# State-space stage of a hybrid encoder kernel: the rounding of the turns and the scaling of the output matrices done on ScalarE in small operations

## The chip, the cores and the metric

One Trainium2 chip, one of its cores. The metric is device time in microseconds (us) for one execution of the whole kernel. Engines are named as in the profile: PE is TensorE (PEld its weight loads), DVE is VectorE, ACT is ScalarE, POOL is GpSimd, SP is SyncE, which here only issues transfers.

## The reference, cut to what matters

The block runs a bidirectional S5 state-space mixer and windowed attention side by side over 272 tokens, merges them by gates, and then runs a product-key expert network. The change is in the state-space mixer alone:

```
def _s5_direction(u_g, a_re, a_im, bb_re, bb_im, c_re, c_im, reverse):
    bu_re = jnp.einsum('lgc,gpc->lgp', u_g, bb_re)
    bu_im = jnp.einsum('lgc,gpc->lgp', u_g, bb_im)
...
    _, _, h_re, h_im = lax.associative_scan(
        _complex_linear_combine, (ar, ai, bu_re, bu_im), reverse=reverse, axis=0)
...
    return jnp.einsum('lgp,gcp->lgc', h_re, cr) - jnp.einsum('lgp,gcp->lgc', h_im, ci)
```

There are 64 groups of 64 states in each of two directions, 8,192 complex states in all. All arithmetic is in 32-bit floats.

## The kernel before, in words

**How the recurrence is turned real.** A complex state that decays by r and turns by an angle at each token is the same as a real recurrence with factor r on inputs that have been turned back by the angle times the token number; the result is turned forward again. So for each set of states the kernel needs the cosine and sine of (turn x token number). The turn is kept in revolutions: ACT multiplies the row of token numbers (`iota`) by the turn per state (tile `tb`), and DVE takes the nearest whole number away, by adding MAGIC (1.5 x 2^23, which leaves only whole numbers) and subtracting it again (tiles `rnd`, `ang`). ACT then makes sine and cosine of `ang` (tile `trig`).

**Tiling.** The 8,192 states stand as 64 columns of 128 partitions. The 1,024 channels are 8 channel tiles (`CT`), with 8 columns each. Columns go in pairs, so there are 32 pairs, 4 for each channel tile (`PPC`), and I call the work on one pair a step. The step function of each engine is unrolled 8 times in `scan_body`; the first body stands by itself, the other three are a hardware loop.

**One step on DVE**, in the order of the code: `pair` (multiply the projected inputs by cosine and sine, L852 and L853; real part of an older pair, L887; add and subtract, L858 and L859; four scans, L868), then `angles` (L838 and L840), `turned_back` (L879 and L880), and in three of the four steps of a channel tile a part of `out_matrices`. That function scales the output matrices C by the coefficients of the tile: four products of 128x256 numbers (L822, L823 in the tile's first step, L825, L826 in its second; tile `cs`), and two differences (L830, L831; tile `cp`) in its third. At a tile's first step stand also `scalars` (L800, L802: the tile's coefficients `scur` and channels `ucur`) and `inputs_low` (L807, L808).

**One step on ACT**: `turns` (L468, L469), `cos_sin` of the pair before (L477, L478, L480), at a tile's first step `inputs_high` (L491, L493), and `gate` (L487), which moves the gate projection of three steps ago out of the accumulator.

**One step on PE**: 8 matmuls of a gate projection (`half_gate`, L1206), the 12 that project the inputs to a pair's states (`state_inputs`, L1252, which wait for the multiplies of the pair before to have read the accumulator, L853), the 6 of `state_outputs` (L1266), and 8 more of the gate projection. In the profile's rows each matmul of L1206 and L1266 counts twice, so a step has 32 of the one and 12 of the other, and 12 of L1252.

**The order** is the order of the code on each engine; the engines meet by counting semaphores. `angles` of a step waits for `turns` of it (`s_tb`). `cos_sin` waits for DVE's `turned_back` of the step before (`s_oc`, `s_os`), and its result (`s_trg`) is used by DVE a step later. PE's `half_gate` waits for ACT's `gate` of two projections before (`s_gs`). SP loads weights into a ring of four, and B and C of a channel tile (`bwt`, `cwt`) ahead of it.

Of the kernel before, what the change touches and what calls it, by code (L numbers as in the profile page):

```python
# [19 lines left out]
ALU = mybir.AluOpType  # L20
ACT = mybir.ActivationFunctionType
AX_X = mybir.AxisListType.X

P = 128
# [3 lines left out]
L = META + SEQ  # L28
# [4 lines left out]
SPC = NST // CT  # L33
# [7 lines left out]
MAGIC = 1.5 * 2.0 ** 23  # L41
# [18 lines left out]
def build(nc, W, keys, par, bw, cw, meta, x, gffn, gfin, u_tab, v_tab, out):  # L60
    top = ExitStack()
    with top:
        def sem(name):
            return top.enter_context(nc.semaphore(name))

        def sbt(stack, name, shape, dt=F32):
            return stack.enter_context(nc.sbuf_tensor(name, shape, dt))
# [17 lines left out]
        hs2 = sbt(top, "hs2", [P, TT, D])  # L85
        st = sbt(top, "st", [P, 16])
        halfpi = sbt(top, "halfpi", [P, 1])


        mix = ExitStack()  # L90
# [17 lines left out]
        scur = sbt(mix, "scur", [P, 2, NSC, SPC])  # L108
# [3 lines left out]
        cwt = sbt(mix, "cwt", [P, 2, SPC, 2, 32])  # L112
# [6 lines left out]
        scan = ExitStack()  # L119
        bwH = sbt(scan, "bwH", [P, 2, 2, 2, P], F32R)  # L120
        cp = sbt(scan, "cp", [P, 2, 2, SPC, 32])
        cs = sbt(scan, "cs", [P, 4, SPC, 32])
        tb = sbt(scan, "tb", [P, 2, 2, L])
        rnd = sbt(scan, "rnd", [P, 2, L])
        ang = sbt(scan, "ang", [P, 2, 2, L])
        trig = sbt(scan, "trig", [P, 2, 2, 2, L])
        pa = sbt(scan, "pa", [P, 2, 2, L])
# [49 lines left out]
        def col(name, a=0, b=None):  # L177
            lo, hi = COLS[name]
            return prm[:, lo + a:hi if b is None else lo + b]

        ident = col("ident")
        iota = col("iota")
# [48 lines left out]
        s_cw = [sem("s_cw0"), sem("s_cw1")]  # L231
        s_scur, s_cpl = sem("s_scur"), sem("s_cpl")
        s_inH, s_inL = sem("s_inH"), sem("s_inL")
        s_cp = sem("s_cp")
        s_bu = sem("s_bu")
        s_tb, s_abs, s_trg, s_rnd = sem("s_tb"), sem("s_abs"), sem("s_trg"), sem("s_rnd")
        s_ang = sem("s_ang")
        s_ab = sem("s_ab")
        s_gin = sem("s_gin")
# [3 lines left out]
        s_y = sem("s_y")  # L243
# [27 lines left out]
        PPC = SPC // 2  # L271
# [6 lines left out]
        def behind(b, t, k):  # L278

            return (b, t - k) if t >= k else (b - 1, t - k + PPL)  # L280
# [5 lines left out]
        def units(t):  # L286

            cc, way, jp = place(t)
            return slice(4 * jp + way, 4 * jp + way + 3, 2)
# [90 lines left out]
        def _(act):  # L380
# [2 lines left out]
            act.sem_inc(s_qT[0], 1)  # L383
            act.sem_inc(s_qT[1], 1)
            act.sem_inc(s_gs, 2)
            act.sem_inc(s_h2T, 4)
            act.sem_inc(s_qp, 2)
            act.sem_inc(s_psc, 2)
# [72 lines left out]
            def turns(b, t):  # L461
                n = PPL * b + t
                cc = t // PPC
                if t % PPC == 0:
                    act.wait_ge(s_scur, 2 * (2 * b + cc) + 2)
                act.wait_ge(s_ang, n + 1)
                at = units(t).start
                nc.scalar.activation(tb[:, t % 2, 0, :], iota, ACT.Copy, scale=scur[:, cc, 0, at:at + 1])  # L468
                nc.scalar.activation(tb[:, t % 2, 1, :], iota, ACT.Copy, scale=scur[:, cc, 0, at + 2:at + 3]  # L469
                                     ).then_inc(s_tb, 1)  # L470

            def cos_sin(b, t):
                s, n = t % 2, PPL * b + t
# [9 lines left out]
            def gate(b, t):  # L483

                g = SPC * b + t
                act.wait_ge(s_wdone, RING + W_GATE + 1 + g)
                nc.scalar.activation(flat(gates_v[:, bass.ds(g, 1), :]), ps[:, t % 2, 0:SEQ], ACT.Identity,  # L487
                                     bias=prm[:, bass.ds(COLS["bgate"][0] + g, 1)]).then_inc(s_gs, 1)

            def inputs_high(b, cc):  # L490
                nc.scalar.activation(uP[:, cc, 0, :], ucur[:, cc, :], ACT.Copy).then_inc(s_inH, 1)  # L491
                act.wait_ge(s_bw[cc], 16 * b + 16)
                nc.scalar.activation(bwH[:, cc, :, :, :].rearrange("p d r s -> p (d r s)"),  # L493
                                     bwt[:, cc, :, :, :].rearrange("p d r s -> p (d r s)"), ACT.Copy).then_inc(s_inH, 1)

            def scan_body(b, first=False):
                for t in range(PPL):
                    turns(b, t)
                    if t >= 1 or not first:
                        cos_sin(*behind(b, t, 1))  # L500
                    if t % PPC == 0:
                        inputs_high(b, t // PPC)
                    if t >= LAG + 1 or not first:
                        gate(*behind(b, t, LAG + 1))

            scan_body(0, first=True)
            with act.Fori(1, BODIES) as b:
                scan_body(b)
# [9 lines left out]
            part = GATES * SEQ // CT  # L518
# [114 lines left out]
        def _(dve):  # L633
# [12 lines left out]
            def step(ins):  # L646

                n_v[0] += 1
                ins.then_inc(s_v, 1)
                dve.wait_ge(s_v, n_v[0])  # L650

            step(nc.vector.memset(halfpi[:, :], HALF_PI))
            nc.vector.memset(st[:, :], 1.0).then_inc(s_ms, 1)

            def low(n, i=0):
# [153 lines left out]
                                        bwt[:, cc, :, :, :].rearrange("p d r s -> p (d r s)"),  # L809
                                        bwH[:, cc, :, :, :].rearrange("p d r s -> p (d r s)"), ALU.subtract).then_inc(s_inL, 1)  # L810

            def out_matrices(b, cc, part):

                ct = 2 * b + cc
                cre, cim = cwt[:, cc, :, 0, :], cwt[:, cc, :, 1, :]

                def co(k):
                    return scur[:, cc, k, :].rearrange("p (i o) -> p i o", o=1).broadcast_to([P, SPC, 32])
                if part == 0:
                    dve.wait_ge(s_cw[cc], 16 * b + 16)  # L820
                    dve.wait_ge(s_cp, 2 * ct + 4)
                    nc.vector.tensor_tensor(cs[:, 0], cre, co(2), ALU.mult).then_inc(s_cpl, 1)  # L822
                    nc.vector.tensor_tensor(cs[:, 1], cim, co(3), ALU.mult).then_inc(s_cpl, 1)  # L823
                elif part == 1:
                    nc.vector.tensor_tensor(cs[:, 2], cre, co(4), ALU.mult).then_inc(s_cpl, 1)  # L825
                    nc.vector.tensor_tensor(cs[:, 3], cim, co(2), ALU.mult).then_inc(s_cpl, 1)  # L826
                else:
                    dve.wait_ge(s_cpl, 4 * ct + 4)
                    dve.wait_ge(s_y, PPC * ct + PPC)
                    nc.vector.tensor_tensor(cp[:, cc, 0], cs[:, 0], cs[:, 1], ALU.subtract).then_inc(s_cp, 1)  # L830
                    nc.vector.tensor_tensor(cp[:, cc, 1], cs[:, 2], cs[:, 3], ALU.subtract).then_inc(s_cp, 1)  # L831

            def angles(b, t):

                s, n = t % 2, PPL * b + t
                dve.wait_ge(s_ang, n + 2)
                dve.wait_ge(s_tb, n + 1)
                nc.vector.tensor_scalar(rnd[:, :, :], tb[:, s, :, :], MAGIC, None, ALU.add).then_inc(s_rnd, 1)  # L838
                dve.wait_ge(s_rnd, n + 1)
                nc.vector.scalar_tensor_tensor(ang[:, s, :, :], rnd[:, :, :], MAGIC, tb[:, s, :, :],  # L840
                                               ALU.subtract, ALU.subtract).then_inc(s_ang, 1)

            def input_products(b, t):
                s, n = t % 2, PPL * b + t
                dve.wait_ge(s_trg, 2 * n + 2)
                dve.wait_ge(s_bu, n + 1 + PPL)
                dve.wait_ge(s_os, n + 2)
                bu = ps[:, 2:6, 0:L].rearrange("p (u r) t -> p u r t", u=2)

                def turn(k):  # L850
                    return trig[:, s, k, :, :].rearrange("p u (o t) -> p u o t", o=1).broadcast_to([P, 2, 2, L])
                nc.vector.tensor_tensor(pa[:, :, :, :], bu, turn(0), ALU.mult).then_inc(s_ab, 1)  # L852
                nc.vector.tensor_tensor(pb[:, :, :, :], bu[:, :, ::-1, :], turn(1), ALU.mult).then_inc(s_ab, 1)  # L853
# [54 lines left out]
            def scan_body(b, first=False):  # L908
                for t in range(PPL):
                    if t % PPC == 0:  # L910
                        scalars(b, t // PPC)
                        if first and t == 0:
                            angles(b, t)
                            inputs_low(b, 0)
                    pair(b, t, first)
                    if t == PPL - 1:
                        take_y(b, 0)
                    if t == PPC - 1 and not first:
                        take_y(b - 1, 1)
                    if not (first and t == 0):  # L920
                        angles(b, t)
                    if t >= 2 or not first:
                        turned_back(*behind(b, t, 2))
                    if t % PPC == 0 and not (first and t == 0):
                        inputs_low(b, t // PPC)
                    if t % PPC < 3:
                        out_matrices(b, t // PPC, t % PPC)

            scan_body(0, first=True)
            with dve.Fori(1, BODIES) as b:  # L930
                scan_body(b)
# [32 lines left out]
            for n in range(W_OUT, W_PQ):  # L964
                c, g = (n - W_OUT) // 4, (n - W_OUT) % 4
# [537 lines left out]
```

## Time and profile before

| | |
|---|---|
| median of 3 runs | 2150.12 us (2145.79 to 2151.93) |
| the profiled execution | 2149.81 us |
| its span, first to last instruction | 2148.0 us |
| mean granted TensorE clock | 0.973 |
| busy: PE 1790.8, DVE 1411.5, POOL 726.3, ACT 399.7 us | 83%, 66%, 34%, 19% of the span |
| state-space stage | from 213 to 574 us of the span |

Busy shares are means over stages with different limits: in the last two thirds of the span, the expert stage, most of the chain is gathers of expert rows from memory. What the change is worth has to be read in the state-space stage alone.

### The profile page before, as it was taken

How to read it: one execution, taken by the hardware profiler on the slowest of the kernel's cores; microseconds unless marked ns; L12 is line 12 of the kernel's file. 1: busy time of each engine (PE TensorE's matmuls, PEld its weight loads, DVE VectorE, ACT ScalarE, POOL GpSimd, SP SyncE). 2: the span in 40 equal slices, each digit the busy share in tenths (PEclk: the TensorE clock that was granted, in tenths of full speed). 3: DMA queues.
4: the chain of work that ended last, by engine and by line, in shares of the span. 5: the costliest groups of instructions: out<-in, count | busy, mean ns of one | idle time of the engine just before them, and what ended most of it. 6: DMA issues, size and time to landing. Idle time of an engine off the chain costs nothing.

```text
span 2148.0 us, 22000 instructions
## 1 busy us (share of the span) xinstructions
PE 1790.8 (83%) x7040; PEld 1086.8 (51%) x7040; DVE 1411.5 (66%) x2293; ACT 399.7 (19%) x783; POOL 726.3 (34%) x558
## 2 busy tenths in 40 slices
PE   6988888998899999977987997777777777777776
PEld 5987666666699885533532553322322322222222
DVE  5535999999755546565565666666766666666654
ACT  4332322322344421110100100001101001000001
POOL 2041000000035004344443455444545544644431
PEclk9999899999999999999998999999999999999999
DMA  4433133223245559999999999999999999999997
GB/s 169 160 125 111 69 108 108 89 106 107 105 170 184 188 213 372 422 421 418 415 417 411 370 397 422 421 422 421 407 422 421 422 422 422 422 422 421 422 421 310
DMA packets 92549, 659.11 MB, mean 307 GB/s; under 512 B 10288, under 2 KB 10288, under 8 KB 12976
## 3 DMA queue, kind: packets, MB, share of 16 engines
q0 software_dynamic: 73728, 536.90, 60.4%
q1 hardware_dynamic: 18752, 121.36, 15.5%
q8 instruction: 34, 0.56, 0.1%
q14 instruction: 35, 0.29, 0.0%
HBM read 656.13 MB, written 2.10 MB: 306 GB/s over the span
## 4 chain that ended last, share of the span: by engine, by line
PE 34%; DMA 30%; DVE 20%; issue 10%; POOL 3%; ACT 1%; DVEq 1%; POOLq 0%; SPq 0%; ACTq 0%
DMA uv<-u_tab,eid 30%; PE ps L1406 14%; DVE pa L868 3%; PE ps L1356 3%; PE ps L1111 3%; PE ps L1113 3%; PE ps L1112 3%; POOL uv L376 2%; DVE uv L1051 2%; DVE pb L853 2%; DVE hs L880 2%; DVE hs L879 2%; PE ps L1339 1%; PE ps L1340 1%; PE ps L1338 1%
## 5 line engine op out<-in xcount | busy, mean ns | idle before, releaser
L1406 PE MATMUL ps<-uv,dg 128*128 128x512 f32 x2048 | 961.1, 615 | 267.4 <-DVE dg L1057 262.6
L1051 DVE CUSTOM_DVE_ANT_0 uv<-uv,xn 128x2048 f32<-128x2048 f32 x256 | 587.0, 2293 | 375.1 <-DMA uv<-u_tab,eid 356.0
L1406 PEld LDWEIGHTS ps<-uv,dg 128*128 128x128 f32 x2048 | 380.4, 194 | 825.9 <-issue 470.4
L376 POOL DMA_INDIRECT uv<-v_tab,eid x256 | 268.1, 1047 | 594.6 <-PE ps L1406 355.8
L373 POOL DMA_INDIRECT uv<-u_tab,eid x256 | 356.5, 1393 | 202.2 <-issue 184.1
L606 ACT ACTIVATE ga<-av 128x1 f32<-128x1 f32 x256 | 51.9, 203 | 1178.7 <-DVE av L1051 1178.7
L1206 PE MATMUL ps<-hT,ring 128*128 128x256 f32 x1024 | 237.0, 390 | 0.0
L1206 PEld LDWEIGHTS ps<-hT,ring 128*128 128x128 f32 x1024 | 196.9, 195 | 42.5 <-issue 15.8
L357 POOL TENSOR_TENSOR fresh<-gated 128x256 f32<-128x256 f32 x16 | 11.8, 739 | 452.2 <-DVE gated L958 452.2
L658 DVE TENSOR_TENSOR low_ring<-ring,wh 128x2048 fp32r<-128x2048 f32 x43 | 107.2, 2499 | 76.6 <-ACT wh L395 76.5
L1057 DVE TENSOR_SCALAR dg<-prm,ga,gw 128x128 f32<-128x128 f32 x256 | 94.5, 369 | 72.3 <-ACT ga L606 31.7
L395 ACT ACTIVATE wh<-ring 128x2048 fp32r<-128x2048 f32 x52 | 99.6, 1914 | 144.8 <-PE ps L1113 106.0
L1356 PE MATMUL ps<-h2T,ring 128*128 128x256 f32 x448 | 100.8, 379 | 0.0
L1356 PEld LDWEIGHTS ps<-h2T,ring 128*128 128x128 f32 x448 | 85.0, 190 | 21.8 <-issue 11.5
L1111 PE MATMUL ps<-hH,wh 128*128 128x272 f32 (+1 forms) x288 | 87.3, 303 | 5.7 <-DVE low_ring L658 4.5
L1112 PE MATMUL ps<-hL,wh 128*128 128x272 f32 (+1 forms) x288 | 84.3, 293 | 0.0
L1113 PE MATMUL ps<-hH,low_ring 128*128 128x272 f32 (+1 forms) x288 | 84.3, 293 | 0.0
L868 DVE TENSOR_TENSOR_SCAN pa<-scur,pa 128x272 f32<-128x272 f32 x128 | 82.0, 701 | 0.0
L351 POOL TENSOR_TENSOR low_ring<-ring,wh 128x2048 fp32r<-128x2048 f32 x8 | 36.6, 4570 | 109.2 <-ACT wh L395 109.2
L1252 PE MATMUL ps<-uP,bwH 32*128 32x272 f32 x256 | 30.6, 326 | 42.6 <-DVE pb L853 38.4
L1111 PEld LDWEIGHTS ps<-hH,wh 128*128 128x128 f32 x288 | 56.7, 197 | 8.0 <-DVE low_ring L658 5.0
L1112 PEld LDWEIGHTS ps<-hL,wh 128*128 128x128 f32 x288 | 56.8, 197 | 0.4
(243 smaller groups left out, 1988.0 us busy)
## 6 DMA issues: line engine op xcount, KB each, us to landing
ring<-W SPq DMA_DIRECT2D x104, 1024.0 KB, 4.8
uv<-u_tab,eid POOLq DMA_INDIRECT x256
uv<-v_tab,eid POOLq DMA_INDIRECT x256
xn<-x SPq DMA_DIRECT2D x2, 1024.0 KB, 6.4
bwt<-bw SPq DMA_DIRECT2D x8, 256.0 KB, 4.7
cwt<-cw SPq DMA_DIRECT2D x8, 256.0 KB, 4.9
out<-xn SPq DMA_DIRECT2D x4, 512.0 KB, 5.3
keyt<-keys SPq DMA_DIRECT2D x1, 1024.0 KB, 7.3
```

The source lines that it names most:

```text
L373: pool.indirect_dma_start(uv[:, s, 0, :], None, u_tab, at).then_inc(s_u[s], 16)
L376: pool.indirect_dma_start(uv[:, s, 1, :], None, v_tab, at).then_inc(s_vv[s], 16)
L395: nc.scalar.activation(high_slot(n), ring[:, n % RING, :], ACT.Copy).then_inc(s_high, 1)
L658: nc.vector.tensor_tensor(low_ring[:, n % RING, :], ring[:, n % RING, :], high_slot(n), ALU.subtract).then_inc(s_low, 1)
L868: nc.vector.tensor_tensor_scan(pa[:, u, k, :], r, pa[:, u, k, :], 0.0, ALU.mult, ALU.add).then_inc(s_gst, 1)
L1051: nc.vector.tensor_tensor_reduce(uv[:, j % UV, 0, :], uv[:, j % UV, 0, :], xn[:, T, :], 1.0, 0.0, ALU.mult, ALU.add, av[:, hh, j:j + 1]).t ...
L1111: nc.tensor.matmul(dst, wh[:, block0 + k, :], xh(k), start=(k == 0), stop=False)
L1112: nc.tensor.matmul(dst, wh[:, block0 + k, :], xl(k), start=False, stop=False)
L1113: ins = nc.tensor.matmul(dst, wl[:, block0 + k, :], xh(k), start=False, stop=(k == last))
L1206: ins = nc.tensor.matmul(ps[:, t % 2, 0:SEQ], w[:, k, :], hTv[:, k, META:L], start=(k == 0), stop=(k == KT - 1))
L1356: ins = nc.tensor.matmul(ps[:, 4 + q % 2, 0:SEQ], w[:, k, :], h2T[:, k, :], start=(k == 0), stop=(k == KT - 1))
L1406: ins = nc.tensor.matmul(ps[:, 4 * T + n, :], dg[:, j % 2, :], uv[:, j % UV, 1, n * 512:(n + 1) * 512], start=False, stop=last and i == 2 ...
```

## The change

In `turns`, ACT now makes two results for each of the two columns of a pair: `tb` as before, and `ang`, the product with MAGIC added. DVE's `angles` loses its first operation (L838) and the tile `rnd`. In a new function `out_products`, ACT makes the four products of the output matrices, each as 8 operations of 128x32 numbers with a scale per partition; DVE keeps only the two differences. The order of the rest stays. ACT's `turns` additionally waits on the counter `s_trg`, for sine and cosine of two pairs before.

```diff
+        magic = sbt(top, "magic", [P, 1])
...
-        rnd = sbt(scan, "rnd", [P, 2, L])
...
+            act.sem_inc(s_trg, 4)
...
-                nc.scalar.activation(tb[:, t % 2, 0, :], iota, ACT.Copy, scale=scur[:, cc, 0, at:at + 1])
-                nc.scalar.activation(tb[:, t % 2, 1, :], iota, ACT.Copy, scale=scur[:, cc, 0, at + 2:at + 3]
-                                     ).then_inc(s_tb, 1)
+                act.wait_ge(s_trg, 2 * n + 2)
+                for u in range(2):
+                    turn = scur[:, cc, 0, at + 2 * u:at + 2 * u + 1]
+                    nc.scalar.activation(tb[:, t % 2, u, :], iota, ACT.Copy, scale=turn)
+                    ins = nc.scalar.activation(ang[:, t % 2, u, :], iota, ACT.Identity, scale=turn, bias=magic[:, :])
+                ins.then_inc(s_tb, 1)
+
+            def out_products(b, cc, k):
+
+                ct = 2 * b + cc
+                if k == 0:
+                    act.wait_ge(s_cw[cc], 16 * b + 16)
+                    act.wait_ge(s_cp, 2 * ct + 4)
+                c, co = ((0, 2), (1, 3), (0, 4), (1, 2))[k]
+                for i in range(SPC):
+                    ins = nc.scalar.activation(cs[:, k, i, :], cwt[:, cc, i, c, :], ACT.Copy, scale=scur[:, cc, co, i:i + 1])
+                ins.then_inc(s_cpl, 1)
...
                     if t % PPC == 0:
                         inputs_high(b, t // PPC)
+                    if t % PPC < 2:
+                        for k in range(2):
+                            out_products(b, t // PPC, 2 * (t % PPC) + k)
...
+            step(nc.vector.memset(magic[:, :], MAGIC))
...
-                if part == 0:
-                    dve.wait_ge(s_cw[cc], 16 * b + 16)
-                    dve.wait_ge(s_cp, 2 * ct + 4)
-                    nc.vector.tensor_tensor(cs[:, 0], cre, co(2), ALU.mult).then_inc(s_cpl, 1)
-                    nc.vector.tensor_tensor(cs[:, 1], cim, co(3), ALU.mult).then_inc(s_cpl, 1)
-                elif part == 1:
-                    nc.vector.tensor_tensor(cs[:, 2], cre, co(4), ALU.mult).then_inc(s_cpl, 1)
-                    nc.vector.tensor_tensor(cs[:, 3], cim, co(2), ALU.mult).then_inc(s_cpl, 1)
...
-                nc.vector.tensor_scalar(rnd[:, :, :], tb[:, s, :, :], MAGIC, None, ALU.add).then_inc(s_rnd, 1)
-                dve.wait_ge(s_rnd, n + 1)
-                nc.vector.scalar_tensor_tensor(ang[:, s, :, :], rnd[:, :, :], MAGIC, tb[:, s, :, :],
+                nc.vector.scalar_tensor_tensor(ang[:, s, :, :], ang[:, s, :, :], MAGIC, tb[:, s, :, :],
                                                ALU.subtract, ALU.subtract).then_inc(s_ang, 1)
...
-                dve.wait_ge(s_trg, 2 * n + 2)
+                dve.wait_ge(s_trg, 2 * n + 6)
...
-                    if t % PPC < 3:
-                        out_matrices(b, t // PPC, t % PPC)
+                    if t % PPC == 2:
+                        out_matrices(b, t // PPC)
```

Three places in the order of instructions follow. First ACT at the very start of the stage, before: the turns of pairs 0 and 1 (L468, L469), channels and B of tile 0 (L491, L493), then the first sine and cosine with the load of the function table.

```order
L468 ACTIVATE tb<-prm,scur 128x272
L469 ACTIVATE tb<-prm,scur 128x272
L491 ACTIVATE uP<-ucur 128x272
L493 ACTIVATE bwH<-bwt 128x512
L468 ACTIVATE tb<-prm,scur 128x272
L469 ACTIVATE tb<-prm,scur 128x272
L477 ACTIVATE trig<-ang 128x544
L478 ACT_TABLE_LOAD
L478 ACTIVATE trig<-ang 128x544
L480 ACTIVATE trig<-trig,halfpi 128x544
```

The same place in the changed kernel, whose lines are numbered anew (L472, L473 are `turns`, L484 is `out_products`, L492 to L495 are `cos_sin`):

```order
L484 ACTIVATE cs<-cwt,scur 128x32 x16
L472 ACTIVATE tb<-prm,scur 128x272
L473 ACTIVATE ang<-prm,magic,scur 128x272
L472 ACTIVATE tb<-prm,scur 128x272
L473 ACTIVATE ang<-prm,magic,scur 128x272
L492 ACTIVATE trig<-ang 128x544
L493 ACT_TABLE_LOAD
L493 ACTIVATE trig<-ang 128x544
L495 ACTIVATE trig<-trig,halfpi 128x544
L484 ACTIVATE cs<-cwt,scur 128x32 x16
```

Sixteen small operations and four more of the turns now stand ahead of the first sine and cosine, and sixteen more behind them.

Second, ACT at a later tile's first step, in the changed kernel:

```order
L492 ACTIVATE trig<-ang 128x544 [waits s_os,s_oc,s_ang]
L493 ACTIVATE trig<-ang 128x544
L495 ACTIVATE trig<-trig,halfpi 128x544 [waits s_abs]
L506 ACTIVATE uP<-ucur 128x272
L508 ACTIVATE bwH<-bwt 128x512 [waits s_bw1]
L484 ACTIVATE cs<-cwt,scur 128x32 [waits s_cp,s_cw1]
L484 ACTIVATE cs<-cwt,scur 128x32 x15
L502 ACTIVATE gates<-ps,prm 128x256 [waits s_wdone]
```

Before, the gate's move (there L487) followed B (L493) at once; now the sixteen small operations stand between them.

Third, DVE at the second step of a tile, before:

```order
L868 SCALAR_TENSOR_TENSOR pa<-scur,pa 128x272 x4
L838 TENSOR_SCALAR rnd<-tb 128x544
L840 SCALAR_TENSOR_TENSOR ang<-rnd,tb 128x544
L879 TENSOR_TENSOR hs<-trig,pa 128x1024
L880 TENSOR_TENSOR hs<-trig,pa 128x1024
L825 TENSOR_TENSOR cs<-cwt,scur 128x256
L826 TENSOR_TENSOR cs<-cwt,scur 128x256
L852 TENSOR_TENSOR pa<-ps,trig 128x1088
```

and in the changed kernel (L872 the scans, L844 the angles, L883 and L884 the turning back, L856 the next pair's first multiply):

```order
L872 SCALAR_TENSOR_TENSOR pa<-scur,pa 128x272 x4
L844 SCALAR_TENSOR_TENSOR ang<-ang,tb 128x544
L883 TENSOR_TENSOR hs<-trig,pa 128x1024
L884 TENSOR_TENSOR hs<-trig,pa 128x1024
L856 TENSOR_TENSOR pa<-ps,trig 128x1088
```

Three instructions of the eight are gone there.

## Rows read from the trace of the kernel before

**Rows 1.** The page's first line.
```profile
span 2148.0 us, 22000 instructions
```
**Rows 2.** A stretch: length; PE, PEld, DVE, ACT, POOL busy; clock, DMA, GB/s.
```profile
342.00:430.00 88.00, 79.54 (x443) 60.25 (x444) 87.08 (x126) 24.84 (x51) 0.00 (x0) 0.94 0.28 97
```
**Rows 3.** Groups, 260 to 540 us: busy us, mean ns | idle before, releaser.
```profile
L852 DVE TENSOR_TENSOR pa<-ps,trig 128x1088 f32<-128x1088 f32 x25 | 32.1, 1284 | 2.0 <-DVE ucur L802 2.0
...
L1252 PE MATMUL ps<-uP,bwH 32*128 32x272 f32 x200 | 22.6, 312 | 29.8 <-DVE pb L853 29.8
...
L480 ACT ACTIVATE trig<-trig,halfpi 128x544 f32<-128x544 f32 x25 | 18.3, 733 | 0.0
...
L477 ACT ACTIVATE trig<-ang 128x544 f32<-128x544 f32 x26 | 17.0, 653 | 150.5 <-DVE hs L880 150.5
...
L478 ACT ACTIVATE trig<-ang 128x544 f32<-128x544 f32 x25 | 16.0, 640 | 0.0
...
L468 ACT ACTIVATE tb<-prm,scur 128x272 f32<-128x272 f32 x25 | 12.8, 512 | 55.4 <-DVE ucur L802 55.4
```
**Rows 4.** Line 852: count, ns min/median/max, first and last start in us.
```profile
L852 DVE TENSOR_TENSOR pa<-ps,trig x32: 1280/1282/1294, 218.8 to 560.2; 128x1088 f32<-128x1088 f32 x32
```
**Rows 5.** DVE in order of time, a second step: start us, us.
```profile
391.72 0.41 DVE L838 TENSOR_SCALAR rnd<-tb 128x544 f32<-128x544 f32 x1
392.17 0.73 DVE L840 SCALAR_TENSOR_TENSOR ang<-rnd,tb 128x544 f32<-128x544 f32 x1
...
395.08 0.42 DVE L825 TENSOR_TENSOR cs<-cwt,scur 128x256 f32<-128x256 f32 x1
395.42 0.42 DVE L826 TENSOR_TENSOR cs<-cwt,scur 128x256 f32<-128x256 f32 x1
395.75 1.28 DVE L852 TENSOR_TENSOR pa<-ps,trig 128x1088 f32<-128x1088 f32 x1
```
**Rows 6.** All engines in order of time, the stage's first microseconds.
```profile
212.98 0.52 ACT L468 ACTIVATE tb<-prm,scur 128x272 f32<-128x272 f32 x1 [5.57 <-DVE ucur L802]
...
213.82 0.41 ACT L491 ACTIVATE uP<-ucur 128x272 fp32r<-128x272 f32 x1
...
214.14 0.61 ACT L493 ACTIVATE bwH<-bwt 128x512 fp32r<-128x512 f32 x1
...
214.66 0.51 ACT L468 ACTIVATE tb<-prm,scur 128x272 f32<-128x272 f32 x1
...
215.48 0.64 ACT L477 ACTIVATE trig<-ang 128x544 f32<-128x544 f32 x1
...
218.00 0.73 ACT L480 ACTIVATE trig<-trig,halfpi 128x544 f32<-128x544 f32 x1
...
218.76 1.29 DVE L852 TENSOR_TENSOR pa<-ps,trig 128x1088 f32<-128x1088 f32 x1
```
**Rows 7.** The page's group of ACT's smallest operation.
```profile
L606 ACT ACTIVATE ga<-av 128x1 f32<-128x1 f32 x256 | 51.9, 203 | 1178.7 <-DVE av L1051 1178.7
```
**Rows 8.** PE in order of time; in brackets the idle time before.
```profile
398.54 0.52 PE L1252 MATMUL ps<-uP,bwH 32*128 32x272 f32 x4
...
400.90 7.17 PE L1206 MATMUL ps<-hT,ring 128*128 128x256 f32 x32
409.07 0.52 PE L1252 MATMUL ps<-uP,bwH 32*128 32x272 f32 x4 [0.99 <-DVE pb L853]
...
420.26 0.52 PE L1252 MATMUL ps<-uP,bwH 32*128 32x272 f32 x4 [1.66 <-DVE pb L853]
...
432.00 0.52 PE L1252 MATMUL ps<-uP,bwH 32*128 32x272 f32 x4 [0.55 <-DVE pb L853]
```
**Rows 9.** A stretch within the slower step; its clock is third from last.
```profile
420.00:425.00 5.00, 4.74 (x29) 3.04 (x30) 4.97 (x10) 2.15 (x6) 0.00 (x0) 0.72 0.00 0
```
**Rows 10.** ACT in order of time, the gate's move in a second step.
```profile
397.03 0.45 ACT L487 ACTIVATE gates<-ps,prm 128x256 f32 x1
```
**Rows 11.** SP in order of time, C of the tile that begins at 417 us.
```profile
396.46 0.33 SPq L319 DMA_DIRECT2D cwt<-cw  x1
```

More of the change, by code:

```diff
@@ L235, in build @@
         s_bu = sem("s_bu")
-        s_tb, s_abs, s_trg, s_rnd = sem("s_tb"), sem("s_abs"), sem("s_trg"), sem("s_rnd")
+        s_tb, s_abs, s_trg = sem("s_tb"), sem("s_abs"), sem("s_trg")
         s_ang = sem("s_ang")
@@ L810, in inputs_low, with out_matrices @@
                                         bwH[:, cc, :, :, :].rearrange("p d r s -> p (d r s)"), ALU.subtract).then_inc(s_inL, 1)
-            def out_matrices(b, cc, part):
+            def out_matrices(b, cc):
                 ct = 2 * b + cc
-                cre, cim = cwt[:, cc, :, 0, :], cwt[:, cc, :, 1, :]
-                def co(k):
-                    return scur[:, cc, k, :].rearrange("p (i o) -> p i o", o=1).broadcast_to([P, SPC, 32])
-                if part == 0:
-                    dve.wait_ge(s_cw[cc], 16 * b + 16)
-                    dve.wait_ge(s_cp, 2 * ct + 4)
-                    nc.vector.tensor_tensor(cs[:, 0], cre, co(2), ALU.mult).then_inc(s_cpl, 1)
-                    nc.vector.tensor_tensor(cs[:, 1], cim, co(3), ALU.mult).then_inc(s_cpl, 1)
-                elif part == 1:
-                    nc.vector.tensor_tensor(cs[:, 2], cre, co(4), ALU.mult).then_inc(s_cpl, 1)
-                    nc.vector.tensor_tensor(cs[:, 3], cim, co(2), ALU.mult).then_inc(s_cpl, 1)
[L827 to L831, printed above, removed]
+                dve.wait_ge(s_cpl, 4 * ct + 4)
+                dve.wait_ge(s_y, PPC * ct + PPC)
+                nc.vector.tensor_tensor(cp[:, cc, 0], cs[:, 0], cs[:, 1], ALU.subtract).then_inc(s_cp, 1)
+                nc.vector.tensor_tensor(cp[:, cc, 1], cs[:, 2], cs[:, 3], ALU.subtract).then_inc(s_cp, 1)
             def angles(b, t):
```

## The prediction

> **What bounds the kernel now.** The change touches one stage, so I first asked which engine sets its length. The busy times by stretch [rows 2] show DVE busy 87.1 of 88 us, PE 79.5 and ACT 24.8. Busy shares alone do not decide, since PE is nearly full too; the idle times before each group do [rows 3]. DVE's first multiply of a step (L852) waited 2.0 us in all in 280 us, and that was for DVE's own copy of the channels. PE waited 29.8 us for DVE's second multiply (L853), ACT 150.5 us for DVE's turning back and 55.4 us for a new tile's scalars. Everybody waits for DVE, and DVE for nobody. The 32 steps' first multiplies start from 218.8 to 560.2 us [rows 4], so a step is (560.2 - 218.8)/31 = 11.01 us, and what leaves DVE shortens it, until another engine is late.
>
> **How close is PE?** From one state projection to the next PE takes 409.07 - 398.54 - 0.99 of waiting = 9.54 us, and 420.26 - 409.07 - 1.66 = 9.53 us, but 432.00 - 420.26 - 0.55 = 11.19 us in the third [rows 8]. In that third one the granted clock was 0.72 over 5 us [rows 9], a mean of the two levels 2.4 and 1.2 GHz; it fell right after the longest of these three waits. Over the 25 steps between 260 and 540 us the wait is 29.8/25 = 1.19 us a step, so PE needs 11.01 - 1.19 = 9.8 us with such dips in it. That is the cover that the gain may use up.
>
> **What is taken from DVE.** L838 to L840 is 392.17 - 391.72 = 0.45 us from start to start, and a product is half of 395.75 - 395.08 = 0.67 us [rows 5]. Starts, not durations (0.41 and 0.42), are what counts, since neighbours overlap on the engine. The operations of the first two steps stand ahead of the first multiply at 218.76 us, where DVE waits for ACT anyway (below), so they give nothing. Behind it lie 30 of the 32 roundings, 30 x 0.45 = 13.5 us, and the four products of tiles 1 to 7, 7 x 2 x 0.67 = 9.4 us. Sum 22.9 us, 0.74 us a step; the step becomes 10.27 us, still 0.45 us over PE's 9.8.
>
> **What is added on ACT.** A turn's operation with a scale from memory starts 0.42 us before the next one (213.82 - 212.98 = 0.84 for two, [rows 6]). The new ones have a second pointer, the bias; no row shows two. One pointer costs 733 - 640 = 0.09 us, which L480 has over L478 on the same shape [rows 3], so I take 0.51 us each, 1.02 us for the two of a pair. (If the second pointer is free: 0.84.)
>
> The small operation of 128x32 with one pointer stands nowhere. Downwards from L491 and L493: 512 instead of 272 columns is 0.61 - 0.41 = 0.20 us, 0.83 ns a column [rows 6]; a 272-column operation with a pointer is 0.51 us, so with 240 columns fewer 0.31 us long, and as each starts 0.10 us before its forerunner's end (0.42 against 0.51), 0.21 us apart. The nearest measured row, 128x1 without a pointer, is 0.203 us long [rows 7]; with the same overlap 0.10 apart is the lower bound. The upper is 0.31, no overlap. I take 0.21: sixteen are 3.4 us (1.6 to 5.0), thirty-two a tile 6.8 us.
>
> In the steady part this is hidden. ACT's tile is then 4 steps of 1.86 (turns), 1.8 (sine and cosine) and 0.4 (gate), plus 0.8 (channels, B) and 6.8, some 24 us of 4 x 10.27 = 41. The turns of a step are made in the step before it or early in it and are used after the scans; the products are used two steps on. What stands behind the sixteen is the gate's move, and PE waits for that: it now starts at 397.03 [rows 10]; with 3.4 us more, 400.4. PE's next gate projection into that buffer begins midway in the 32 gate matmuls that start at 400.90 [rows 8], at 400.9 + 3.6 = 404.5, so 4 us of cover is left, 2.5 at the upper price; in a tile's first step it is 1.0 less, since there the turns stand ahead of it too. C is no wait either: for the tile that starts at 417 it is issued at 396.46 [rows 11]. A single memset at the kernel's start lies under the first load.
>
> **What lands on the path.** At the stage's start ACT is ahead of DVE: DVE's first multiply at 218.76 follows ACT's last sine or cosine, 218.00 + 0.73 [rows 6], and the order there shows what moves ahead of it. Turns of pair 0: +1.02. Then L491 and L493, then sixteen small ones: +3.4. Turns of pair 1: +1.02. The rest, with the table load, stays (215.48 to 218.76). The first multiply is late by 5.4 us, at 224.2. Bounds: 0.84 + 1.6 + 0.84 = 3.3 to 1.02 + 5.0 + 1.02 = 7.0 us. Behind it come sixteen more and the turns of pair 2, 3.4 + 1.9 = 5.3 us on ACT; DVE needs those turns after its pair, some 6.3 us later. About 1 us is left; at the upper price DVE waits 0.6 us there.
>
> **The sum.** -22.9 + 5.4 = -17.5 us, with the bounds -19.6 to -15.3. The profiled execution took 2149.8 us, 1.8 over its span of 2148.0 [rows 1], and 0.3 under the median of 2150.1. So 2132.3 by the profile, 2132.6 by the median. What follows the stage waits for its last output, and its weights are loaded ahead, so it moves as a block.
>
> **A rule that speaks against the change.** The products cost DVE 4 x 0.34 = 1.35 us a tile and will cost ACT 6.8 [rows 5, 6]. The Trainium skill says the same as advice (ScalarE: Activation LUTs, Rules for kernel authors): additions and multiplications belong on VectorE. By that rule the time would not come down, and it is right on the work; the trace disagrees on the time, since ACT idles 206 of 280 us [rows 3]. The rule would win from the point at which ACT's tile fills 41 us, (41 - 17)/32 = 0.75 us for a small operation.
>
> **Rivals.**
> - ACT is dearer than taken (chance 0.15). With 0.4 us for a small operation, twice my price, the start costs 6.4 + 2.0 = 8.4 us, the turns of pair 2 make DVE wait 2 us more, and the gate's move comes just when PE needs it. -22.9 + 10.4 = -12.5: 2137.5 us. For it: no row of this kernel shows many ACT operations of this size in a row. Against: the 203 ns of L606.
> - The gain is taken by someone else (0.10). PE is the candidate: it would need 10.8 us a step instead of 9.8, or ACT's saturation as above. Then a step stays near 10.8 and 0.2 x 30 = 6 us of gain meet 5.4 of loss: 2150 us, no change.
> - Slower, by TensorE's clock (0.05). A dip costs 11.19 - 9.54 = 1.65 us and comes about once in a tile now. If it came in every step, PE would need 9.54 + 1.65 = 11.2 us and be the bound: 30 x 0.2 + 5.4 = 11 us more, 2161 us. It decides from 10.85 us a step, four dips in five steps. For it: PE has longer to wait at the start (5 us), and works in shorter rounds. Against: the dips follow the long waits, and the waits shrink. The Trainium skill states (TensorE: Matmul & The Clock Gate, Part 1) that the clock is halved when the array has lately been idle and full when it is busy; rows 8 and 9 agree, and by it this rival should not come.
> - The forecast (0.70), with its own range of 2129 to 2136.
>
> **How the numbers follow.** The three runs scatter by 3 us about their middle, and 0.3%, 6.5 us, is about what a measurement tells from no change, so faster means under 2143.7. Forecast and dear ACT lie there, 0.85, and a sliver of a half-eaten gain; the eaten gain is the same, slower 0.05. The range takes in the bounds of the forecast, the scatter and the dear ACT: 2127 to 2141, which leaves out the last two rivals.
>
> **What would show it.** In the profile after: DVE without L838 and the four products; 128x32 operations on ACT of about 0.31 us, 0.21 apart; the first multiply at 224 us instead of 218.8; the last one at 560.2 + 5.4 - 22.9 = 542.7; PE's wait for L853 down from 1.19 to about 0.45 us a step; no wait of DVE for ACT after 235 us. Wrong would be shown by waits of DVE's multiplies for PE or ACT in the steady part, waits of PE for ACT's gate, more table loads in the stage, or a granted clock well under 0.94.

## The result and the profile after

The changed kernel takes 2130.32 us (median of 4, 2127.96 to 2133.57), the kernel before in the same runs 2148.94 us. The ratio is 0.9915, 95% interval 0.9893 to 0.9936, so 18.3 us less (13.8 to 23.0). The profiled execution took 2133.57 us with a span of 2131.7, against 2149.81 and 2148.0 [rows 1].

The stretches of the state-space stage, with the columns of [rows 2]: us; PE, PEld, DVE, ACT, POOL busy; clock, DMA share, GB/s.

```profile
262.00:342.00 80.00, 73.47 (x436) 57.06 (x436) 79.10 (x106) 45.20 (x128) 0.00 (x0) 1.00 0.34 119
342.00:430.00 88.00, 81.43 (x476) 63.41 (x471) 87.14 (x117) 49.51 (x137) 0.00 (x0) 1.00 0.30 108
```

In the 88 us from 342 to 430 us ACT's busy time doubled, from 24.8 to 49.5, and DVE is as full as it was, 87.1. So DVE is still the bound, only its steps are shorter. One thing I had not counted on: TensorE's clock is 1.00 where it was 0.94.

The groups that answer to [rows 3], here from 255 to 530 us (busy us, mean ns | idle before, releaser):

```profile
L484 ACT ACTIVATE cs<-cwt,scur 128x32 f32<-128x32 f32 x208 | 45.4, 308 | 0.0
...
L856 DVE TENSOR_TENSOR pa<-ps,trig 128x1088 f32<-128x1088 f32 x27 | 34.7, 1287 | 2.7 <-DVE ucur L821 2.0
...
L473 ACT ACTIVATE ang<-prm,magic,scur 128x272 f32<-128x272 f32 x52 | 31.3, 602 | 0.0
...
L1256 PE MATMUL ps<-uP,bwH 32*128 32x272 f32 x216 | 24.2, 310 | 20.8 <-DVE pb L857 20.7
...
L492 ACT ACTIVATE trig<-ang 128x544 f32<-128x544 f32 x26 | 17.0, 653 | 62.5 <-DVE hs L884 62.5
```

The new small operation (L484) is 308 ns long, the operation with two pointers (L473) 602. DVE's first multiply (L856) waits for no other engine. PE's wait for the second multiply fell from 29.8 us in 25 steps to 20.8 in 27, that is from 1.19 to 0.77 a step. ACT still idles.

Line 856, as [rows 4]:

```profile
L856 DVE TENSOR_TENSOR pa<-ps,trig x32: 1279/1290/1293, 224.0 to 543.1; 128x1088 f32<-128x1088 f32 x32
```

The first is at 224.0 us, the last at 543.1, so 31 steps take 319.1 us instead of 341.4: 22.3 us less. The start of the stage, as [rows 6], ACT and then DVE in order of time:

```profile
212.82 0.52 ACT L472 ACTIVATE tb<-prm,scur 128x272 f32<-128x272 f32 x1 [5.57 <-DVE ucur L821]
...
215.51 3.48 ACT L484 ACTIVATE cs<-cwt,scur 128x32 f32<-128x32 f32 x16
218.90 0.51 ACT L472 ACTIVATE tb<-prm,scur 128x272 f32<-128x272 f32 x1
...
223.25 0.73 ACT L495 ACTIVATE trig<-trig,halfpi 128x544 f32<-128x544 f32 x1
...
220.93 0.73 DVE L844 SCALAR_TENSOR_TENSOR ang<-ang,tb 128x544 f32<-128x544 f32 x1 [4.25 <-ACT ang L473]
224.01 1.29 DVE L856 TENSOR_TENSOR pa<-ps,trig 128x1088 f32<-128x1088 f32 x1 [2.35 <-ACT trig L495]
```

Sixteen small operations take 218.90 - 215.51 = 3.39 us, and DVE waits through them, 4.25 and 2.35 us. From the copy of the first scalars to the first multiply it is 11.61 us instead of 6.20, 5.4 more. Together: -22.3 + 5.4 = -16.9 us. The stage's last output reaches ACT at 555.2 us instead of 572.3, and what follows takes 1576.5 us, before 1575.7: it moved as a block.

### The profile page after: what moved, and what is told of

Same layout as the page of the kernel before. It is cut to its first block and busy times, and to the rows that moved or that the text cites. A ratio compares the mean times of both kernels' runs of the same rounds, so it can differ in the third digit from the quotient of the medians.

```text
span 2131.7 us, 22309 instructions
## 1 busy us (share of the span) xinstructions
PE 1772.2 (83%) x7040; PEld 1079.0 (51%) x7040; DVE 1386.9 (65%) x2230; ACT 485.7 (23%) x1103; POOL 711.5 (33%) x558
## 3 DMA queue, kind: packets, MB, share of 16 engines
q1 hardware_dynamic: 18752, 121.36, 15.7%
## 5 line engine op out<-in xcount | busy, mean ns | idle before, releaser
L1410 PE MATMUL ps<-uv,dg 128*128 128x512 f32 x2048 | 951.4, 609 | 275.4 <-DVE dg L1061 269.9
L373 POOL DMA_INDIRECT uv<-u_tab,eid x256 | 339.0, 1324 | 202.1 <-issue 185.8
L1210 PE MATMUL ps<-hT,ring 128*128 128x256 f32 x1024 | 232.0, 385 | 0.0
L1360 PEld LDWEIGHTS ps<-h2T,ring 128*128 128x128 f32 x448 | 85.0, 190 | 21.8 <-issue 11.5
L872 DVE TENSOR_TENSOR_SCAN pa<-scur,pa 128x272 f32<-128x272 f32 x128 | 82.0, 701 | 0.0
## 6 DMA issues: line engine op xcount, KB each, us to landing
uv<-v_tab,eid POOLq DMA_INDIRECT x256, 14.3
```

Source lines behind the costliest of these rows:

```text
L373: pool.indirect_dma_start(uv[:, s, 0, :], None, u_tab, at).then_inc(s_u[s], 16)
L1210: ins = nc.tensor.matmul(ps[:, t % 2, 0:SEQ], w[:, k, :], hTv[:, k, META:L], start=(k == 0), stop=(k == KT - 1))
L1360: ins = nc.tensor.matmul(ps[:, 4 + q % 2, 0:SEQ], w[:, k, :], h2T[:, k, :], start=(k == 0), stop=(k == KT - 1))
L1410: ins = nc.tensor.matmul(ps[:, 4 * T + n, :], dg[:, j % 2, :], uv[:, j % UV, 1, n * 512:(n + 1) * 512], start=False, stop=last and i == 2 ...
```

## The experiments

Each kernel was timed beside the kernel before, whose median there was 2152.35 us in the first four experiments, 2151.39 in 5, 6 and 8, and 2150.75 in 7 and 9. An edit is shown against the changed kernel unless said otherwise. Since the times of one kernel scatter by a few us, I also read each profiled run in two stretches: *start* is from the copy of the first scalars (`scur`) to the first multiply of the stage (before 6.20 us, in the change 11.61), *steps* is from there to the last step's first multiply (before 341.4 us, in the change 319.1).

**1. The rounding alone.** ACT adds MAGIC; the products stay DVE's.

```diff
-                    if t % PPC < 2:
-                        for k in range(2):
-                            out_products(b, t // PPC, 2 * (t % PPC) + k)
...
+                    nc.vector.tensor_tensor(cs[:, 0], cre, co(2), ALU.mult).then_inc(s_cpl, 1)
+                    nc.vector.tensor_tensor(cs[:, 1], cim, co(3), ALU.mult).then_inc(s_cpl, 1)
```

> Half of the change alone: the added MAGIC is ACT's, the four products of the output matrices stay on DVE. Theory 1 (the gain is DVE's starts behind its first multiply, the loss is what ACT does ahead of it): 30 roundings of 0.45 us leave, 13.5 us, and two pairs of extra turns, 2.0 us, come ahead of the first multiply. First multiply at 218.6 + 2.0 = 220.6 us, the last at 560.2 + 2.0 - 13.5 = 548.7 us, the time 11.5 us under the kernel before. Theory 2 (the stage is shorter because TensorE's clock dips less, 0.973 to 0.982 in the profiled runs, and DVE's work is incidental): the split between the halves would not follow the counts of DVE's operations, and the clock would move with the time.

**2. The products alone.**

```diff
-                    ins = nc.scalar.activation(ang[:, t % 2, u, :], iota, ACT.Identity, scale=turn, bias=magic[:, :])
...
+                nc.vector.tensor_scalar(rnd[:, :, :], tb[:, s, :, :], MAGIC, None, ALU.add).then_inc(s_rnd, 1)
```

> The other half alone: the products are ACT's, the rounding stays on DVE. Theory 1: seven tiles lose 2 x 0.67 us on DVE, 9.4 us, and sixteen small operations, 3.4 us, come ahead of the first multiply. First multiply at 218.6 + 3.4 = 222.0 us, the last at 560.2 + 3.4 - 9.4 = 554.2 us, the time 6.0 us under before; with the rounding alone the two halves add up to the whole change, 17.5 us. Theory 2: no such sum.

Line of the first multiply in each of the two:

```profile
L866 DVE TENSOR_TENSOR pa<-ps,trig x32: 1274/1284/1293, 217.4 to 544.5; 128x1088 f32<-128x1088 f32 x32
```
```profile
L855 DVE TENSOR_TENSOR pa<-ps,trig x32: 1279/1290/1293, 220.0 to 554.0; 128x1088 f32<-128x1088 f32 x32
```

The rounding alone: start 8.22 us (+2.02, expected 2.0), steps 327.1 (-14.3, expected -13.5), time 2134.53, ratio 0.9927 (0.9911 to 0.9944), by which 15.7 us less, where 11.5 was expected and the stage alone gives 12.3. The rest lies ahead of the stage in the profiled execution: its first scalars came at 209.2 us instead of 212.6, behind a stretch from 110 to 160 us in which the clock was 1.00 and not 0.97; nothing of the change is there. The products alone: start 9.59 us (+3.39, expected 3.4), steps 334.0 (-7.4, expected -9.4), time 2143.29, ratio 0.9958 (0.9942 to 0.9975), 9.0 us less by the ratio, where 6.0 was expected and the stage alone gives 4.0. Its first scalars came at 210.4 us, 2.2 us early; the other 3 us are not placed, and are about the scatter of the runs.

The starts add up, 2.02 + 3.39 = 5.41, as the change has it. The steps do almost: 14.3 + 7.4 = 21.7 against 22.3. The sum is what theory 1 wants, and every step shortens only where DVE lost an operation. The clock does not decide between the theories by itself: in the four profiled executions it rises as the time falls (before 0.973, products 0.975, rounding 0.979, both 0.982), as theory 2 also says. Against theory 2 stand DVE's waits, since no first multiply of the stage waits for PE in any of the four, and experiment 5 below, whose clock is 0.975 with steps as short as the change's. But the products are worth 2 us less alone than I had said. The steps of that kernel show where: a tile's first step falls by 0.67 us as computed (11.74 to 11.07), its second by 0.13 to 0.48 (10.78 to 10.30 at best). In three of the seven second steps the first multiply waited for the turning back before it, 0.9 us in all; why in these three only stays open.

**3. The first tile's products back on DVE; 4. and the first two roundings too.** The second edit comes on top of the first.

```diff
-                    if t % PPC < 2:
+                    if t % PPC < 2 and not (first and t < PPC):
...
+                    if first and t < 2:
+                        first_products(t)
```
```diff
+                if first and t < 2:
+                    for u in range(2):
+                        ins = nc.scalar.activation(tb[:, t % 2, u, :], iota, ACT.Copy, scale=scur[:, cc, 0, at + 2 * u:at + 2 * u + 1])
+                    ins.then_inc(s_tb, 1)
+                    return
```

> The changed kernel, but the products of the first channel tile are DVE's again (four operations of 128x256 in the time in which DVE waits for ACT's first sine and cosine); tiles 1 to 7 as in the change. Theory 1: the sixteen small operations leave the way to the first multiply, which comes at 220.6 instead of 224.0 us, and everything behind moves with it: the last at 539.7 instead of 543.1 us, the time 3.4 us under the changed kernel. Rival (the start's loss is made good anyway, since PE needs 9.8 us of the step's 10.3 and would be late by as much): the first multiply comes earlier, the last one does not.

> As the run with the first tile's products on DVE, and the rounding of the first two pairs is DVE's again too, so that the start of the stage is that of the kernel before. Theory 1: the first multiply at 218.6 us, the last at 560.2 - 22.9 + 0.3 = 537.6 us or a few tenths under, the time 5.4 us under the changed kernel and 22.9 us under before. Rival: as in the run before, the start's gain is lost again behind it.

```profile
L867 DVE TENSOR_TENSOR pa<-ps,trig x32: 1276/1290/1293, 220.1 to 539.2; 128x1088 f32<-128x1088 f32 x32
```
```profile
L879 DVE TENSOR_TENSOR pa<-ps,trig x32: 1276/1290/1294, 218.0 to 537.1; 128x1088 f32<-128x1088 f32 x32
```

Start 8.22 and 6.20 us, steps 319.1 in both, the same as in the change: every microsecond taken from the start is kept, so PE does not eat it. The start is 3.39 us shorter than the change's in the first and 5.41 in the second, which is the price of ACT's work there, to the hundredth. The times are 2129.78 (ratio 0.9892, 0.9875 to 0.9908) and 2126.21 us (0.9882, 0.9866 to 0.9899). The last is the fastest kernel that computes everything; against the change's 0.9915 the intervals just overlap, and the difference is shown by the profile (last first multiply at 537.1 instead of 543.1 us), not by the measured times alone.

**5. and 6. The small operations twice and three times**, in tiles 1 to 7, on top of 3.

```diff
                 ins.then_inc(s_cpl, 1)
+                for again in spare:
+                    for i in range(SPC):
+                        nc.scalar.activation(again(k, i), cwt[:, cc, i, c, :], ACT.Copy, scale=scur[:, cc, co, i:i + 1])
```

> The kernel with the first tile's products on DVE, and in tiles 1 to 7 every small operation on ACT is done twice (the second into a spare tile that nobody reads): 64 instead of 32 a tile. It prices the cover. Theory 1 (a deadline, not a sum, decides): ACT's turns of a tile's third pair are ready some 24 us after the tile's scalars, DVE wants them at 27.3 us, so DVE does not wait and the last multiply stays at 539.7 us. The gate's move of the second step comes some 3 us after PE wants it, so PE waits for ACT a few us a tile, which it gets back from its waits for DVE. Rival (the work costs on ACT what it costs, the rule that products belong on VectorE): each tile is longer by 6.8 us, the last multiply at 587 us.

> The same with every small operation three times, 96 a tile. ACT's work is then 17 + 20 = 37 us of a tile's 41, still under it. Theory 1: the turns of the third pair are ready at 31 us after the scalars, DVE wants them at 27.3, so it waits 3.7 us once a tile for ACT's last turn operation, 26 us in seven tiles; the last multiply near 566 us. Rival (only ACT's sum counts, 0.75 us for an operation): still no wait. Second rival (PE's wait for the gate's move is what stops DVE, through the state inputs): DVE's waits would be in front of the first multiply, released by PE.

The steps with twice and with three times:

```profile
L873 DVE TENSOR_TENSOR pa<-ps,trig x32: 1278/1291/1293, 219.4 to 538.6; 128x1088 f32<-128x1088 f32 x32
```
```profile
L873 DVE TENSOR_TENSOR pa<-ps,trig x32: 1278/1292/1294, 217.5 to 571.4; 128x1088 f32<-128x1088 f32 x32
```

Waits of PE with twice, 230 to 545 us (us in total, times, longest):

```profile
PE ps L1229 <- ACT gates L508: 18.5, 12, 2.2
PE ps L1275 <- DVE pb L874: 3.3, 1, 3.3
```

and with three times, of DVE (213 to 590 us) and of PE (230 to 545):

```profile
DVE ang L861 <- ACT ang L476: 23.6, 8, 3.7
DVE pa L873 <- PE ps L1275: 10.1, 7, 2.4
```
```profile
PE ps L1229 <- ACT gates L508: 39.8, 13, 5.5
```

Twice: steps 319.2 us, nothing lost (time 2129.82 us, ratio 0.9899), though ACT is busy for 47 us more than in 3 (526.2 against 479.0). PE now waits for ACT's gate move, 18.5 us in all, and for DVE only once, near the start, as expected: the wait changed its releaser. Three times (one execution, 2166.9 us): steps 353.9 us, 34.8 more where I expected 26. The wait for the turns is there, and the second rival's wait as well: 10.1 us in front of the first multiply, released by PE, whose own wait for the gate's move had reached 39.8 us. ACT was busy 80.1 of the 100 us from 430 to 530, so its sum was still under the tile, and the rival that only sums is out.

**7. The gate's move ahead of the triple operations.** This separates the two. The edit is shown against the kernel with three times.

```diff
+                    if t >= LAG + 1 or not first:
+                        gate(*behind(b, t, LAG + 1))
                     if t % PPC < 2 and not (first and t < PPC):
                         for k in range(2):
                             out_products(b, t // PPC, 2 * (t % PPC) + k)
-                    if t >= LAG + 1 or not first:
-                        gate(*behind(b, t, LAG + 1))
```

> The kernel with every small operation three times, but the gate's move stands ahead of them. With three times, DVE waited 23.6 us for ACT's turns and 10.1 us for PE, while PE waited 39.8 us for ACT's gate move. Theory A (two separate deadlines behind the sixteen): PE's waits for the gate's move go, and with them DVE's 10.1 us for PE; DVE's wait for the turns stays at 3.7 us a tile; first multiplies span 353.9 - 10 = 344 us. Rival (one cause, ACT is simply full): 354 us as before, the waits only change their name.

```profile
L873 DVE TENSOR_TENSOR pa<-ps,trig x32: 1278/1290/1293, 217.8 to 563.5; 128x1088 f32<-128x1088 f32 x32
```
```profile
DVE ang L861 <- ACT ang L476: 26.0, 8, 3.8
DVE pa L873 <- DVE ucur L827: 2.0, 6, 0.4
```
```profile
PE ps L1229 <- ACT gates L508: 27.6, 7, 4.1
```

DVE's wait for PE is gone, that for the turns stays, steps 345.7 us (expected 344), the time of one execution each 2153.6 instead of 2166.9 us. In each of tiles 1 to 7 one step is 14.1 or 14.2 instead of 10.3 us, which is about the 3.7 us that the deadline of the third pair's turns gives. But the expectation also said that PE's waits for the gate's move would go, and that was wrong: 7 of 13 are left, 27.6 of 39.8 us, one in a tile of up to 4.1 us. That one falls in the step in which DVE waits for the turns as well, since the third step's gate move still stands behind them and behind the small operations of the second step. So what is shown is that DVE loses time in two ways, some 26 us by the turns and 8.2 (353.9 - 345.7) by the gate's moves of a tile's first two steps; the deadline of the gate's move was not removed altogether.

**8. Less work on DVE: what is the next bound?** This kernel leaves out most of three operations in each step, and its output is not the reference's. It stands on top of 4; one of the three is not shown here.

```diff
-                nc.vector.tensor_tensor(pa[:, :, 0, :], pa[:, :, 0, :], pb[:, :, 0, :], ALU.add).then_inc(s_gin, 1)
+                nc.vector.tensor_tensor(pa[:, :, 0, 0:16], pa[:, :, 0, 0:16], pb[:, :, 0, 0:16], ALU.add).then_inc(s_gin, 1)
```

> What comes next when DVE has less to do. The kernel with the start of the one before, and three of DVE's operations of every step (real part, add, subtract) work on 16 columns instead of 256 or 272, so this kernel leaves out most of that arithmetic and its output is not the reference's. DVE's step falls by some 1.4 us, from 10.27 to 8.9. Theory 1 (PE is the next bound at 9.54 us, 9.8 with dips of its clock): the step stops at 9.6 to 9.8 us, DVE waits for PE's state inputs, the last multiply at 218.6 + 31 x 9.7 = 519 us. Rival (PE's need is mostly waiting in disguise): the step goes on to 8.9 us, the last multiply at 495 us.

The steps, then DVE and PE in order of time (idle before in brackets):

```profile
L879 DVE TENSOR_TENSOR pa<-ps,trig x32: 1281/1292/1294, 218.1 to 505.2; 128x1088 f32<-128x1088 f32 x32
```
```profile
400.96 1.29 DVE L879 TENSOR_TENSOR pa<-ps,trig 128x1088 f32<-128x1088 f32 x1 [1.26 <-PE ps L1281]
...
410.44 1.29 DVE L879 TENSOR_TENSOR pa<-ps,trig 128x1088 f32<-128x1088 f32 x1 [0.60 <-PE ps L1281]
```
```profile
399.90 0.53 PE L1281 MATMUL ps<-uP,bwH 32*128 32x272 f32 x4
...
409.37 0.52 PE L1281 MATMUL ps<-uP,bwH 32*128 32x272 f32 x4
```

The first ten steps take 8.3 to 9.3 us while PE falls behind; from then on each takes 9.4 to 9.6, mostly 9.47, DVE waits for PE's state inputs and PE for nobody. The last first multiply is at 505.2 us: between my 519 and the rival's 495, because I had left out the ten steps in which PE's lateness only builds up, and because PE needs 9.47 and not 9.7 us. Its clock was 1.00 from 300 to 506 us. One execution took 2101.3 us.

**9. The turning back ahead of the angles**, on top of 4 and shown against it, for the 1.4 to 2 us that the products fell short.

```diff
-                    if not (first and t == 0):
-                        angles(b, t, first)
                     if t >= 2 or not first:
                         turned_back(*behind(b, t, 2))
+                    if not (first and t == 0):
+                        angles(b, t, first)
```

> The kernel with the start of the one before, and in every step DVE's turning back is put ahead of the angles. In the changed kernel a tile's second step takes 9.82 instead of 10.78 us, 0.96 less, though the rounding (0.48) and two products (0.67) left it. Theory A: the next first multiply overwrites what the turning back still reads, so directly behind it it starts 1.32 us after it instead of 1.13 behind another operation; with the angles in between, the second steps fall by 0.19 us, in seven tiles by 1.3 us, and the first multiplies span 317.8 us instead of 319.1. Rival: the 0.19 us are PE's or ACT's lateness; then nothing changes or the steps grow, since ACT is released for the next sine and cosine at the same or a later time.

First the changed kernel, a tile's second step, then this one, and its steps:

```profile
383.26 2.56 DVE L872 TENSOR_TENSOR_SCAN pa<-scur,pa 128x272 f32<-128x272 f32 x4
385.74 0.70 DVE L844 SCALAR_TENSOR_TENSOR ang<-ang,tb 128x544 f32<-128x544 f32 x1
...
387.49 1.21 DVE L884 TENSOR_TENSOR hs<-trig,pa 128x1024 f32<-128x1024 f32 x1
388.81 1.29 DVE L856 TENSOR_TENSOR pa<-ps,trig 128x1088 f32<-128x1088 f32 x1
```
```profile
378.34 2.56 DVE L895 TENSOR_TENSOR_SCAN pa<-scur,pa 128x272 f32<-128x272 f32 x4
381.02 1.22 DVE L906 TENSOR_TENSOR hs<-trig,pa 128x1024 f32<-128x1024 f32 x1
382.16 1.22 DVE L907 TENSOR_TENSOR hs<-trig,pa 128x1024 f32<-128x1024 f32 x1
383.30 0.72 DVE L867 SCALAR_TENSOR_TENSOR ang<-ang,tb 128x544 f32<-128x544 f32 x1
383.93 1.28 DVE L879 TENSOR_TENSOR pa<-ps,trig 128x1088 f32<-128x1088 f32 x1
```
```profile
L879 DVE TENSOR_TENSOR pa<-ps,trig x32: 1279/1283/1293, 217.6 to 539.2; 128x1088 f32<-128x1088 f32 x32
```

In the change the next first multiply starts 1.32 us after the last turning back (388.81 - 387.49). Here the angles start 1.14 behind the turning back and the multiply 0.63 behind the angles, as behind any other operation: the 0.19 us there are gone. But the turning back now starts 381.02 - 378.34 = 2.68 us after the first scan, where the angles started 2.48 after it in the change (385.74 - 383.26), since it reads what the last scan writes (the code makes it wait there for the counter of the scans). A tile's second step stays at 9.8 us, its first and third grow by 0.13 to 0.23, steps 321.6 us instead of 319.1: slower by 2.5 where I expected 1.3 faster. The fourth step is a control: there another DVE operation (tile `yT`) stands between scans and turning back in both kernels, no gap opens behind the scans, and the step stays at 10.7 to 10.8 us. The cause I had named, a wait for one's own predecessor, is borne out by both places; the forecast for the swap was wrong, because the angles had been hiding such a wait behind the scans already. Time 2129.36 us, ratio 0.9909 (0.9892 to 0.9926).

## Why the prediction was right

The forecast was 2132.3 us by the profile and 2132.6 by the median, and its range of 2127 to 2141 holds the measured 2130.32; the forecast case was the one that came. Step by step:

- **DVE bounds the stage, and what leaves it shortens it.** Right: experiments 1 to 4, and experiment 8 shows the point where it ends.
- **30 x 0.45 for the roundings.** 14.3 us instead of 13.5, 0.48 each: besides the 0.45 that L838 took, the angles are 0.70 instead of 0.73 us long. Small, and to the good.
- **7 x 2 x 0.67 for the products.** Mis-sized: on top of the rounding they gave 22.3 - 14.3 = 8.0 us, not 9.4. In a tile's second step two products give 0.48 us and not 0.67, because they had also been filling a wait: the next first multiply writes `pa`, which the turning back before it still reads. I counted starts that are freed and did not ask what the next instruction would then stand behind. Alone, without the other half, they gave 7.4.
- **22.9 us in all.** 22.3 measured; the two errors go against each other, and that the sum is nearer than its terms is luck.
- **5.4 us at the start.** 5.41 measured, and its parts 2.02 and 3.39. The price of the small operation, 0.31 us long and 0.21 apart, extrapolated from columns and pointers, is what the trace shows (308 ns and 3.39/16 = 0.21). The Trainium skill (ScalarE: Activation LUTs, What ACT_TABLE_LOAD costs) has a formula for it, 186 ns plus 0.833 ns a column plus 93 ns for each pointer operand: by it the estimates are 306 ns, and 599 ns for the turns with two pointers; the trace agrees, 308 and 602.
- **The stage's start needs 1 us of cover for the third pair's turns.** Right: no wait of DVE there.
- **The gate's move has 4 us of cover.** Right in kind: no wait in the change, waits of up to 2.2 us at double the work, and a loss to DVE only at three times. The size was too large: double work is 3.4 us more in each of the two steps, against a cover of 4 us, 3 in a tile's first step, so PE should have waited 0.4 us at most.
- **PE needs 9.8 us a step and would keep 0.45 us.** The size was wrong: it keeps 0.77 us, since PE needs 9.5. I had taken the clock's dips as part of its need. Before, each of the six dips from 262 to 530 us came behind a wait of 1.65 to 2.19 us (three waits of 1.65 to 1.73 us had none); in the change no wait there is above 1.3 us and no dip is left, clock 0.94 before and 1.00 after in the same 88 us. That is the opposite of the slower rival. The Trainium skill's rule (TensorE: Matmul & The Clock Gate, Part 1), halved when lately idle and full when busy, agrees with these stretches in kind.
- **What follows moves as a block.** Right, 1575.7 and 1576.5 us.
- **The rule that speaks against the change.** The rule of the Trainium skill (ScalarE: Activation LUTs, Rules for kernel authors), that additions and multiplications belong on VectorE, holds for the work: ACT spends 6.8 us on a tile's products, DVE spent 1.35. On the time it does not hold here: 8 us came out of them in the steps, 3.4 were lost at the start, and even at double the work nothing more was lost.

The measured difference of the medians, 18.6 us, is above the 16.9 of the stage; the profiled runs differ by 16.2. The rest is within the scatter of the runs, so that the median came out so near the forecast says little about the last two microseconds. What stays open is why a stretch ahead of the stage runs at a clock of 0.97 in some executions and 1.00 in others, worth up to 3 us; the changed kernel has the same instructions there, but for one memset at the very start.

## What to carry to other kernels

When one engine bounds a stage, price a move by the starts it frees behind the point where that engine really begins to bound, and put the price of the receiving engine against its deadlines (which of its results is wanted when), not against its sum: here ACT could do twice the moved work for nothing and lost 35 us at three times. Look separately at the stage's first steps, where the receiving engine is the one waited for; undoing the move for the first tile's products and the first two roundings won 5.4 us more. And before removing or moving an operation, look whether the one that comes to stand behind its neighbour depends on it, because the removed one may have been hiding a wait.

## What the runs showed of the hardware

- On DVE an operation that has to wait for its direct predecessor starts 0.1 to 0.2 us later than one that hasn't: 1.32 instead of 1.13 us behind the turning back, 2.59 to 2.69 instead of 2.48 behind the scans. Before the change it shows too, behind the rounding [rows 5]: L840 starts 0.04 us after L838's end (392.17 against 391.72 + 0.41), where a neighbour that doesn't depend starts 0.08 before it. The Trainium skill (Perfetto Trace Analysis, Optimizing Scalar/DVE Operations) says that the part of an instruction in which its write is acknowledged overlaps with the next one; it fits that this overlap, 0.08 us here, is lost when the next one has to wait. The other 0.11 us behind the turning back come after its end (388.81 against 387.49 + 1.21), and what fills them no run shows.
- With shorter waits of PE its clock rose from 0.94 to 1.00 in the stage, while its work stayed the same; no run changes the waits alone. A need measured over stretches with dips overstates what PE needs once it is kept busy, 9.8 against 9.47 us.
